# First attention: heads 0 to 7 placed between the projection pieces of the second halves of q, k and v, and the bias laid out by the input

## The reference

```python
def chunked_band_attention(h, w_qkv, w_o, rel_table):
    """h: (B,S,D). Each frame attends to its own chunk and the 8 previous chunks."""
    qkv = jnp.einsum('bsd,de->bse', h, w_qkv).reshape(B, S, 3, N_HEADS, HEAD_DIM)
    ...
    rel = qi + pad - kj
    idx = jnp.clip(rel, -MAX_REL_DIST, MAX_REL_DIST) + MAX_REL_DIST
    bias = rel_table[:, idx].astype(jnp.float32)
    ...
        s = jnp.einsum('bqhd,bkhd->bhqk', q_c, k_band).astype(jnp.float32) * scale + bias
        s = jnp.where(key_pos[None, None, None, :] >= 0, s, NEG_INF)
        p = jax.nn.softmax(s, axis=-1).astype(v_band.dtype)
        return jnp.einsum('bhqk,bkhd->bqhd', p, v_band)
    ...
    return jnp.einsum('bsd,de->bse', o, w_o)
```

## Time and profile before

| | |
|---|---|
| median of 3 runs | 1271.43 us (1270.32 to 1274.81) |
| profiled execution | 1273.82 us, its span 1272.0 us |
| busy, TensorE | 1102.6 us (87%) |
| busy, GpSimd | 698.1 us (55%) |
| busy, ScalarE | 528.9 us (42%) |
| busy, VectorE | 502.9 us (40%) |
| mean granted TensorE clock | 0.91 |
| longest share of the chain that ended last | PE, 33% |

### The profile page before, as it was taken

How to read it: one execution, slowest core, us unless ns; L and a number is a source line. 1 busy time by engine, 2 the same in 40 slices (tenths; PEclk the granted TensorE clock), 3 DMA queues, 4 the chain that set the end, 5 groups by cost and what they waited for, 6 DMA issues and landing times. The chain is left out here.

```text
span 1272.0 us, 19774 instructions
## 1 busy us (share of the span) xinstructions
PE 1102.6 (87%) x8448; PEld 917.8 (72%) x8448; DVE 502.9 (40%) x678; ACT 528.9 (42%) x797; POOL 698.1 (55%) x309
## 2 busy tenths in 40 slices
PE   6989999999977689999969996898787879976686
PEld 5878889899876679999954453798666558854554
DVE  1023236432147635321235236435474450037532
ACT  5444364445434656444521131222431564453251
POOL 6981068998845488988820025000376739981060
PEclk9995699999988889999989998899897889986688
DMA  9940055555534345555562342000044535530140
GB/s 361 322 149 1 20 169 178 193 187 185 196 117 148 134 132 171 191 185 188 190 202 83 115 165 83 3 5 4 3 133 151 176 113 189 195 116 1 46 161 33
DMA packets 47767, 171.46 MB, mean 135 GB/s; under 512 B 5088, under 2 KB 7392, under 8 KB 47488
## 3 DMA queue, kind: packets, MB, share of 16 engines
q1 hardware_dynamic: 45232, 161.15, 37.8%
q0 software_dynamic: 2448, 9.05, 2.1%
HBM read 169.13 MB, written 4.19 MB: 136 GB/s over the span
## 5 line engine op out<-in xcount | busy, mean ns | idle before, releaser
L624 POOL TENSOR_TENSOR ring_r<-ring,high_r 128x1024 fp32r<-128x1024 f32 x256 | 638.0, 2521 | 256.6 <-ACT high_r L755 255.7
L755 ACT CAST high_r<-ring 128x1024 fp32r<-128x1024 f32 x256 | 265.1, 1049 | 269.3 <-DMA ring<-w 269.0
L389 PE MATMUL psum<-x_high,high_r 128*128 128x256 f32 x640 | 182.7, 285 | 1.6 <-DVE x_low L261 1.6
L389 PE MATMUL psum<-x_low,high_r 128*128 128x256 f32 x640 | 181.6, 284 | 0.0
L389 PE MATMUL psum<-x_high,ring_r 128*128 128x256 f32 x640 | 181.4, 283 | 0.0
L374 PE MATMUL psum<-high_r,x_high 128*128 128x512 f32 x320 | 128.5, 401 | 8.9 <-POOL ring_r L624 5.4
L374 PE MATMUL psum<-ring_r,x_high 128*128 128x512 f32 x320 | 127.6, 399 | 0.0
L374 PE MATMUL psum<-high_r,x_low 128*128 128x512 f32 x320 | 127.0, 397 | 0.0
L389 PEld LDWEIGHTS psum<-x_high,high_r 128*128 128x128 f32 x640 | 123.3, 193 | 2.9 <-issue 2.3
L389 PEld LDWEIGHTS psum<-x_low,high_r 128*128 128x128 f32 x640 | 123.3, 193 | 0.6
L536 DVE TENSOR_TENSOR arena<-arena 128x512 f32<-128x512 f32 x32 | 46.1, 1440 | 196.2 <-ACT arena L512 196.1
(11 more groups left out here) (309 smaller groups left out, 1775.8 us busy)
## 6 DMA issues: line engine op xcount, KB each, us to landing
ring<-w SPq DMA_DIRECT2D x292, 512.0 KB, 3.3
row<-rows POOLq DMA_DIRECT2D x14, 512.0 KB, 8.3
bias_spread<-relt SPq DMA_DIRECT2D x1, 3072.0 KB, 13.7
arena<-bias_spread SPq DMA_DIRECT2D x1, 2048.0 KB, 9.7
h<-x SPq DMA_DIRECT2D x1, 1024.0 KB, 5.1
arena<-lora POOLq DMA_DIRECT2D x2, 512.0 KB, 6.9
out<-h SPq DMA_DIRECT2D x1, 1024.0 KB, 4.0
con<-consts SPq DMA_DIRECT2D x1, 529.0 KB, 4.9
```

The costliest lines, as they stand in the source:

```text
L389: ins = nc.tensor.matmul(out, a, b, start=(k == 0 and q == 0), stop=(k == KT - 1 and q == 2))
L624: nc.gpsimd.tensor_tensor(low(m), raw(m), read(high(m)), ALU.subtract).then_inc(low_made, 1)
L755: nc.scalar.copy(high(m), raw(m)).then_inc(high_made, 1)
```

## The change

**Order on TensorE.** Tiles 0 to 2 (the first halves) run as before, but the transposes of their q and k stand between the pieces of tile 2, in two pairs of banks (`pe_transpose_pair`). Then TensorE waits for their copies and starts the attention. Turns 0 to 7 of the loop hold the 12 pieces of tiles 3 to 5 between their scores and their transposes, 2, 1, 1, 2, 2, 2, 1 and 1 of them (`FILL`). Turns 4 to 7 begin with the transposes of the second halves of q and k, one bank each (`PAIR_AT`, now all in bank 3). Turns 8 to 18 hold heads only. ScalarE and VectorE evacuate tiles 3, 4 and 5 inside their own loops over the heads (`TILE_AT`, L519 and `project_dve`).

**Banks.** Tile 2 uses banks 0 and 1, tile 3 banks 2 and 3, tiles 4 and 5 banks 0 and 1. The four groups of head outputs go to banks 2, 3, 0 and 1.

**Splits.** ScalarE's casts in the attention follow the pieces used: seven ahead in turns 0 to 7, then up to piece 31.

**T_O.** Each bank of transposes of the output waits for its own group of four heads, no longer for all four groups.

**Bias.** The input now holds the bias as it is used, 128x16x384. SyncE loads heads 0 to 7 ahead of piece 8 and heads 8 to 15 ahead of piece 12. GpSimd sets the masked columns with two fills for each half and copies nothing.

```diff
+        QKV_BANK = [0, 2, 0, 2, 0, 0]
+        O_BANK = [2, 3, 0, 1]
+
+        FILL = [2, 1, 1, 2, 2, 2, 1, 1]
+        FILLED = [sum(FILL[:hh]) for hh in range(len(FILL) + 1)]
+        TILE_AT = {2: 3, 4: 4, 7: 5}
+        PAIR_AT = {4: (0, 0, 2), 5: (1, 0, 3), 6: (2, 1, 2), 7: (3, 1, 3)}
...
-                split_until(min(4 * W_O + 1 + hh, 4 * W_O + 8))
+                split_until(4 * W_QKV + 12 + FILLED[min(hh, 8)] + (7 if hh < 8 else 8))
...
+                if hh + 1 in PAIR_AT and PAIR_AT[hh + 1][0] % 2 == 0:
+                    i, which, b = PAIR_AT[hh + 1]
+                    evacuate_pair(act, T_K, i, (qT, kT)[which], b)
+                if hh + 1 in TILE_AT:
+                    project_act(act, TILE_AT[hh + 1])
...
+                if m in (8, 12):
+
+                    half = slice(8 * (m == 12), 8 * (m == 12) + 8)
+                    sp.dma_start(bias[:, half, :], relt[:, half, :]).then_inc(bias_ready[m == 12], 16)
...
-                if m == 9:
-
-
-                    sp.dma_start(spread, bass.AP(relt.tensor, 0, [[0, P], [1, HEADS * 384]])).then_inc(spread_stored, 16)
...
-            pe_linear(pe, W_QKV, 6, xT2, qkv_free, transposed(pe, T_H0))
-            pe.wait_ge(con_landed, 16)
-            pe.wait_ge(qkv_act, 6)
-            pe.wait_ge(qkv_dve, 6)
-            pe_transposes(pe, T_Q, qn)
-            pe_transposes(pe, T_K, kn)
-            evacuated(pe, T_K)
...
+            qkv_out(1)
+            for i in range(4):
+                qkv_piece(2, i)
+                if i == 0:
+                    for b in range(2):
+                        pe_transpose_pair(pe, T_Q, b, qn, b)
+                if i == 1:
+                    qkv_out(2)
+                    for b in range(2):
+                        pe_transpose_pair(pe, T_Q, 2 + b, kn, b)
+            bank_out(pe, 4 * T_Q + 3)
             for hh in range(HEADS + 3):
...
+                if hh in PAIR_AT:
+
+                    i, which, b = PAIR_AT[hh]
+                    qkv_out(4 + which)
+                    pe_transpose_pair(pe, T_K, i, (qn, kn)[which], b)
+                if hh < 8:
+                    for n in range(FILLED[hh], FILLED[hh + 1]):
+                        if n % 4 == 0:
+
+                            qkv_out((2, 3, 5)[n // 4])
+                        qkv_piece(3 + n // 4, n % 4)
...
-            pe.wait_ge(o_ready, 4)
-            pe_transposes(pe, T_O, on)
+            pe_transposes(pe, T_O, on, lambda b: pe.wait_ge(o_ready, b + 1))
```

More of the change, by code:

```diff
@@ L182, in build @@
             for _b in range(4):
-                bank_ = 4 + _b if _i in SPLIT_T else 6 + _b % 2
+                bank_ = 4 + _b if _i in SPLIT_T else 3 if _i == T_K else 6 + _b % 2
                 BANK_OF.append(bank_)
@@ L209, in pe_transposes, with pe_transpose_pair, evacuate_pair @@
                 ins.then_inc(tp_filled, 1)
+        def pe_transpose_pair(pe, inst, i, src, b):
+            g = 4 * inst + i
+            if PREVIOUS[g] is not None:
+                bank_out(pe, PREVIOUS[g])
+            for j in range(2):
+                for t in range(NT):
+                    ins = nc.tensor.transpose(psum[:, BANK_OF[g], (2 * j + t) * P:(2 * j + t + 1) * P],
+                                              src[:, t, (2 * b + j) * P:(2 * b + j + 1) * P], ident)
+            ins.then_inc(tp_filled, 1)
+        def evacuate_pair(eng, inst, i, dst, b):
+            g = 4 * inst + i
+            eng.wait_ge(tp_filled, g + 1)
+            dd = dst[:, 2 * b:2 * b + 2, :]
+            if i % 2 == 0:
+                nc.scalar.copy(dd, filling(g)).then_inc(tp_act, 1)
+            else:
+                nc.vector.tensor_copy(dd, filling(g)).then_inc(tp_dve, 1)
         def filling(g):
@@ L353, in transposed, with pe_piece @@
             return lambda i: bank_out(pe, 4 * inst + i)
+        def pe_piece(pe, n, i, bank, lhs):
+            m = 4 * n + i
+            for t in range(NT):
+                tt = slice(t * P, (t + 1) * P)
+                for j in range(2):
+                    k = 2 * i + j
+                    if n in PLAIN:
+                        pairs = ((lhs[:, k, tt], raw(m, 2, HALF)[:, j, :]),)
+                    else:
+                        pairs = parts([x_[:, k, tt] for x_ in lhs], (high(m, 2, HALF)[:, j, :], low(m, 2, HALF)[:, j, :]))
+                    for q, (a, b) in enumerate(pairs):
+                        ins = nc.tensor.matmul(psum[:, bank + t, :], a, b, start=(k == 0 and q == 0),
+                                               stop=(k == KT - 1 and q == len(pairs) - 1))
+            ins.then_inc(piece_used, 1)
         def pe_chunk(pe, n, c, lhs, banks_free, ready=None):
             for i in range(4):
-                m = 4 * n + i
-                piece_ready(pe, m)
+                piece_ready(pe, 4 * n + i)
                 if ready is not None:
@@ L364, in pe_chunk @@
                     banks_free(pe, c)
[L365 to L376, removed]
+                pe_piece(pe, n, i, 2 * (c % 2), lhs)
         def pe_linear(pe, first, chunks, lhs, banks_free=None, ready=None):
@@ L632, in _ @@
                 load_row(r)
[L633 to L639, removed]
+            for i, until in ((0, 14), (1, 20)):
+                low_until(until)
+                pool.wait_ge(bias_ready[i], 16)
+                nc.gpsimd.memset(bias[0:64, 8 * i:8 * i + 8, 192:256], -1e30)
+                nc.gpsimd.memset(bias[0:64, 8 * i:8 * i + 8, 320:384], -1e30).then_inc(mask_set, 1)
             low_until(4 * W_RKVG)
@@ L765, in _ @@
             moments(0)
[L767 to L775, removed]
+            split_for(W_QKV)
+            act.wait_ge(rstd_ready, 1)
+            project_act(act, 0)
+            split_for(W_QKV + 1)
+            project_act(act, 1)
+            evacuate_pair(act, T_Q, 0, qT, 0)
+            split_for(W_QKV + 2)
+            project_act(act, 2)
+            evacuate_pair(act, T_Q, 2, kT, 0)
             attention_act(act, split_until)
@@ L1074, in _ @@
             rms(0)
[L1075 to L1080, removed]
-                    evacuate(dve, inst, b, dst)
-            dve.wait_ge(con_landed, 16)
-            dve.wait_ge(mask_set, 1)
+            project_dve(dve, 0)
+            project_dve(dve, 1)
+            evacuate_pair(dve, T_Q, 1, qT, 1)
+            project_dve(dve, 2)
+            evacuate_pair(dve, T_Q, 3, kT, 1)
             for hh in range(HEADS + 3):
                 if hh < HEADS:
+                    if hh % 8 == 0:
+                        dve.wait_ge(mask_set, hh // 8 + 1)
                     dve.wait_ge(sc_done, hh + 1)
```

58 lines of the change are left out of this document (42 added, 16 removed).

## The result

| | before | after |
|---|---|---|
| median, same chip | 1270.88 us (4 runs, 1270.12 to 1274.81) | **1242.76 us** (4 runs, 1241.29 to 1243.34) |
| profiled execution, its span | 1273.82, 1272.0 | 1243.18, 1241.4 |
| mean granted clock | 0.91 | 0.925 |
| TensorE busy | 1102.6 us | 1075.8 us |

The ratio is 0.9757, 95% interval 0.9735 to 0.9778: 28.1 us less by the medians, 30.6 by the two profiled executions. The forecast was 1244.5, 26.9 less.

A forecast was written before the change was run, and what follows sets the result against it. TensorE itself was taken as the bound, mostly at half clock from 84.23 to 151.69 us. Terms summed to 40.5 us in place of 67.46, a gain of 27.0 against the 1271.43 median: 1244.5 us, range 1240 to 1258.

The forecast's parts named there:

- (a): The 32 transposes of q and k, placed between projection pieces that cover their copies: 4.0 us, between 3.4 and 4.8.
- (b): New TensorE wait before head 0 for the k copies, which stand behind the evacuation of tile 2: 1.6 us.
- (c): The 16 attention heads at full clock, 1.85 us each instead of 3.58: 29.6 us, range 28.6 to 33.6.
- (e): TensorE's wait at head 8, because ScalarE casts pieces 30 and 31 ahead of its exponentials: 1.1 us, zero at half clock.
- (f): End of the head loop, where TensorE waits for softmax and a copy: about 0.6 us, zero at half clock.
- (d): Slower first steps at changes between kinds of matmul, two borders in each of eight turns: 1.6 us, zero at best.
- (g): Output transposes before W_O, each bank waiting only for its own four heads: 2.0 us at full clock, now 4.2.
- disputed term: Clock in heads 8 to 15, which run bare: forecast to hold full clock once it is already up.
- Rival 1: Clock falls again behind the last projection piece, slowing the bare heads: about 1254.5, to 1258 us; chance 0.32.
- Rivals 2 and 3: Interleaving holds TensorE up, about 1256 us, chance 0.08; clock falls inside heads 0 to 7, about 1288 us, chance 0.04.

The follow-up runs named there:

- experiment 3: Kernel of experiment 2 plus 12 useless dense matmuls, six ahead of each of turns 1 and 2 of the head loop: 1243.14 us, ratio 0.9764.
- experiment 6: Changed kernel with TensorE held ahead of turn 8 by three useless GpSimd fills: 1263.29 us, ratio 0.9924.
- experiment 5: Kernel before with only 12 useless dense matmuls added, six ahead of each of turns 1 and 2: 1249.82 us, ratio 0.9817.
- experiment 2: Changed kernel without interleaving: six projection tiles first, q and k transposes between pieces of the last two, then 16 bare heads: 1266.91 us, ratio 0.9954.
- experiment 8: Changed kernel with the scores of two heads issued side by side on TensorE's upper and lower 64 rows: 1239.18 us, ratio 0.9733.

## Why the prediction came out as it did, and what failed in it

All terms, from start to start. The measured column is what comes on top of the projection matmuls until W_O, as in the forecast:

| term | forecast | measured | from |
|---|---|---|---|
| (a) transposes of q and k | 4.0 | 3.2 | 32 of them, summed between starts |
| (b) wait ahead of head 0 | 1.6 | 1.7 | 52.07 to 53.99, less a matmul's 0.226 |
| (c) 16 heads | 29.6 | 30.7 | all steps of the heads, without the waits in (e) and (f); 1.94 a bare turn |
| (d) borders between kinds | 1.6 | 1.5 | 12 first steps of 0.31 to 0.34 make 1.2, the slower ones behind them 0.3 |
| (e) ScalarE's casts ahead of head 8 | 1.1 | 0.45 | row at 107.10 |
| (f) end of the loop | 0.6 | 0.5 | row at 119.28, and 0.2 |
| (g) T_O | 2.0 | 2.1 | 121.11 to 123.21 |
| sum | 40.5 | 40.1 | |

The sum can be had in another way. From the first projection matmul to W_O it was 135.67 us before (16.02 to 151.69) and is 107.11 now. Of the 28.56 difference 1.2 is the earlier full clock at the start, which leaves 27.4 for the change, against 27.0 forecast. The rest up to 28.1 by the medians is within the drift of the code behind.

**The step that failed in size** is term (c), the price of a head at full clock. The prediction took 1.85 us, 29.6 for 16. It measured 1.94 and 30.7. The prediction scaled a head by halving and by the ratio of the 256-column scores in the earlier trace rows. But the steps from one kind of matmul to the next shrink less: from the 128-column scores to the transposes it is 0.56 us at half clock (118.49 to 119.05 in the earlier trace rows) and 0.32 at full (110.75 to 111.07). (e) is too large by 0.65: ScalarE was through with head 8's exponentials 6.2 us behind piece 23 (100.82 to 107.03), not 6.6, and TensorE came to the transposes after 5.8, not 5.5. (a) is too large by 0.8, and 3.2 lies below its own range of 3.4 to 4.8. The row says less than 0.107 a transpose: 1.03 less 0.3 is 0.73 for eight, and they took 0.79 here. The errors have both signs, so that the sum is within 0.4 us is partly luck.

**The disputed term** came out as forecast, but the reasons given for it failed. For heads 0 to 7 it was that the pieces in each turn are the dense work which holds the clock. That was not needed: no turn of experiment 3 behind turn 2 has any. For heads 8 to 15 it was the row from 84.4 to 91.0, as the nearest one at full clock. That row ends two us ahead of the fall, in the kernel before:

```profile
93.00:94.00 1.00, 0.51 (x2) 0.42 (x3) 0.96 (x4) 0.00 (x0) 0.00 (x0) 0.84 0.00 0
94.00:95.00 1.00, 0.98 (x4) 0.59 (x2) 0.97 (x4) 0.88 (x4) 0.00 (x0) 0.50 0.00 0
```

```profile
93.49 1.07 PE L1537 MATMUL psum<-arena 64*128 64x256 f32 x2 [0.71 <-DVE arena L1091]
```

The clock fell behind the transposes and at the waits of the loop's first scores (0.87 us in the earlier trace rows, then 0.71), before heads had followed one another without a gap. This could have been read ahead of time, and the prediction did not read it. It held only that "this mix of short matmuls does not raise the clock; whether it holds a clock that is already up, no row shows". Experiment 3 shows that it holds it, through 16 heads; experiment 6 that it doesn't raise it after a pause. What counts is the start of the loop: either no gap opens there, or dense work behind the gap brings the clock back, as in experiment 5.

The Trainium skill (TensorE: Matmul & The Clock Gate, What's actually happening) says that activity releases the throttle. Experiments 2 and 6 disagree as the kernel before did, with 46.0 us at 0.51 and 28.0 us at 0.50 of unbroken work. The Trainium skill (TensorE: Matmul & The Clock Gate, HAM oscillation — how this bites in real kernels) lays a clock that falls to idle gaps of TensorE. Experiment 6 agrees, with one of 4.71 us, and in experiment 2 gaps of 0.74 and 1.66 us between short work were enough.

**The rivals.** Rival 1 did not come: the clock was 1.00 in heads 8 to 15. Had it come, the pause of experiment 6 shows that its price was of the right size: 1263.3, of which 4.7 us are the pause itself, so about 1258.6 against the 1254.5 to 1258 worked out. Its chance of 0.32 was fair for what the prediction had read: whether the heads hold the clock no row of the kernel before shows, and experiment 3 does. Rivals 2 and 3 did not come either: TensorE waited for no split, and no piece ran at half clock.

**A cost that stayed hidden, as forecast.** The prediction put the first half of the bias at "some 4 us of transfer at worst". On the page of the changed kernel its two halves of 1536 KB took 14.6 us from issue to landing (median). That is more than the transfer alone, but it is what the cover has to hide, and 19 us were enough: TensorE waits for no piece among the heads.

**What I left out.** A gap that a change opens costs its own length and the clock behind it. I priced the new wait (b) at 1.6 us only, and it was safe: the clock stayed at 1.00. That this is due to the dense pieces on both sides of it is an inference; no run tests it. In experiment 2 I made the mistake in earnest: my own theory gave it the changed kernel's time and left the start of the loop out. It lost 24 us with gaps of 2.4.

## What to carry over

Before a stretch of short matmuls that follows dense ones, look at its first two turns: a pipeline that is still empty leaves gaps there, and the clock that falls in them may not come back while the mix lasts. Fill these gaps with work that is due anyway (one or two dense pieces a turn), or with a few useless matmuls where there is none, and test with exactly such matmuls whether the clock is what a stretch lacks before anything is moved. Once the clock is up, the next bound is near: here the copy of k ahead of head 0 (1.53 us) and the exponentials with the casts ahead of them on ScalarE (waits of 0.45 to 1.42 us).

## What the runs showed of the hardware

- The same mix of short matmuls runs at either clock for as long as it lasts: 53.5 us at 0.50 in the kernel before, 30 us at 1.00 in experiment 3. Its busy share is nearly the same in both (53.3 of 53.5 and 29.7 of 30). Which of the two it ran at was settled in the first turns of the loop.
- Twelve useless matmuls of 512 columns, some 2.7 us of work, took 24 us off in both kernels: 1266.9 to 1243.1, and 1273.95 to 1249.8 (single runs of the latter 1245 to 1256).
- Two 64-row score matmuls of two heads, on the upper and the lower 64 rows and one behind the other, take 0.54 us together for 256 columns, the time of one (experiment 8).
- The clock fell within an idle gap of 4.71 us (experiment 6) and at gaps of 0.74 and 1.66 us with short matmuls between them (experiment 2). It stayed at 1.00 over one of 1.53 us between dense matmuls (the changed kernel).
- The code behind the change ran up to 3 us faster or slower in stretches of equal work, as the clock fell at other points (58.5 us at 0.94 and 55.3 at 0.97).
